# Two-layer decoder trunk on one core: FFN gate/up projection of steps 1 to 10 with the weights stationary and the tokens moving

## What is computed

```python
for l in range(2):
    x = x + 0.5 * swiglu(rmsnorm(x, norm_ffn1[l]), w1_gate[l], w1_up[l], w1_down[l])
    p = rmsnorm(x, norm_mix[l]) @ w_in[l]            # 1024 x 3072
    x = x + concat(diff_attention(p), retention(p)) @ w_out[l]
    x = x + 0.5 * swiglu(rmsnorm(x, norm_ffn2[l]), w2_gate[l], w2_up[l], w2_down[l])
return rmsnorm(x, norm_final)
# swiglu(h, g, u, d) = (silu(h @ g) * (h @ u)) @ d ;  g, u: 1024 x 2816 ;  d: 2816 x 1024
```

## Time and profile before

| | us |
|---|---|
| median of 3 runs | 993.77 (993.65 to 994.35) |
| profiled execution, first to last instruction (span) | 992.8 |
| TensorE busy in it | 965.0 (4512 matmuls) |
| VectorE / ScalarE busy | 547.3 / 455.8 |
| mean granted TensorE clock | 0.998 of full |

### The profile page before, as it was taken

One profiled execution on the slowest core, in us unless ns is written; L12 is line 12 of the kernel. 1 busy time (PEld: TensorE's weight loads), 2 busy tenths in 40 slices (PEclk: granted clock), 3 DMA queues, 4 the chain that ended last, 5 costly groups with the idle time before them and its releaser, 6 DMA issues.

```text
span 992.8 us, 12951 instructions
## 1 busy us (share of the span) xinstructions
PE 965.0 (97%) x4512; PEld 796.2 (80%) x4512; DVE 547.3 (55%) x628; ACT 455.8 (46%) x579; POOL 39.7 (4%) x73
## 2 busy tenths in 40 slices
PE   2999999999999999999999999999999999999997
PEld 2888888888888888888878888888888888888885
DVE  3654545565666645454655545456565755454454
ACT  3634344454573534343453434343655554343432
POOL 3400000000010000000000000000001000000000
PEclk9999999999999999999999999999999999999999
DMA  9664646447245655556536655656634645656541
GB/s 251 219 208 160 208 161 206 171 160 241 91 164 170 205 199 172 208 169 211 188 131 214 188 193 175 205 171 210 209 110 165 213 134 189 212 165 207 164 141 43
DMA packets 123179, 178.70 MB, mean 180 GB/s; under 512 B 5664, under 2 KB 95776, under 8 KB 123136
## 3 DMA queue, kind: packets, MB, share of 16 engines
q1 hardware_dynamic: 121808, 173.56, 52.4%
q0 software_dynamic: 1040, 3.54, 1.5%
q10 hardware_dynamic: 288, 1.05, 0.3%
HBM read 177.08 MB, written 1.05 MB: 179 GB/s over the span
## 4 chain that ended last, share of the span: by engine, by line
PE 95%; DMA 1%; ACT 1%; issue 1%; DVE 1%; SPq 0%; ACTq 0%; POOLq 0%; DVEq 0%; POOL 0%
PE gu L722 20%; PE gu L724 20%; PE gu L723 20%; PE acc L724 10%; PE acc L723 10%; PE acc L722 10%; PE tp L792 2%; DMA raw<-in_w_up_dram 1%; PE tp L737 1%; PE tp L840 1%; PE acc L851 1%; PE tp L863 1%; ACT w_hi L294 0%; ACT wide L394 0%; PE acc L863 0%
## 5 line engine op out<-in xcount | busy, mean ns | idle before, releaser
L478 DVE TENSOR_TENSOR w_lo<-raw,w_hi 128x2048 fp32r<-128x2048 f32 (+1 forms) x168 | 376.2, 2243 | 158.5 <-ACT w_hi L294 158.3
L722 PE MATMUL gu<-w_hi,xT_hi 128*128 128x512 f32 x896 | 353.1, 394 | 11.4 <-DVE w_lo L478 11.0
L724 PE MATMUL gu<-w_hi,xT_lo 128*128 128x512 f32 x896 | 350.2, 391 | 0.0
L723 PE MATMUL gu<-w_lo,xT_hi 128*128 128x512 f32 x896 | 349.7, 390 | 0.0
L294 ACT ACTIVATE w_hi<-raw 128x2048 fp32r<-128x2048 f32 (+1 forms) x168 | 313.8, 1872 | 21.8 <-DMA raw<-in_w_up_dram 11.4
L722 PEld LDWEIGHTS gu<-w_hi,xT_hi 128*128 128x128 f32 x896 | 168.8, 188 | 46.7 <-issue 12.3
L336 ACT ACTIVATE hid<-gu,st 128x256 f32<-128x256 f32 x88 | 41.8, 475 | 352.2 <-PE gu L724 352.1
L724 PEld LDWEIGHTS gu<-w_hi,xT_lo 128*128 128x128 f32 x896 | 168.7, 188 | 35.7
L723 PEld LDWEIGHTS gu<-w_lo,xT_hi 128*128 128x128 f32 x896 | 168.9, 189 | 34.1
L722 PE MATMUL acc<-w_hi,aT_hi 128*128 128x512 f32 x384 | 157.0, 409 | 0.0
L534 DVE SCALAR_TENSOR_TENSOR hid<-gu,st,hid 128x256 f32<-128x256 f32 x88 | 42.5, 483 | 205.3 <-ACT hid L336 205.3
(11 more groups left out here) (111 smaller groups left out, 396.4 us busy)
## 6 DMA issues: line engine op xcount, KB each, us to landing
raw<-in_w_gate_dram SPq DMA_DIRECT2D x88, 512.0 KB, 4.0
raw<-in_w_up_dram SPq DMA_DIRECT2D x88, 512.0 KB, 5.0
raw<-in_w_down_dram SPq DMA_DIRECT2D x88, 512.0 KB, 4.3
raw<-in_w_in_dram SPq DMA_DIRECT2D x40, 512.0 KB, 4.6
raw<-in_w_out_dram SPq DMA_DIRECT2D x16, 512.0 KB, 3.7
raw<-in_w_in_dram SPq DMA_DIRECT2D x16, 256.0 KB, 3.0
gain<-in_norm_ffn_dram POOLq DMA_DIRECT2D x3, 512.0 KB, 4.0
gain<-in_norm_mix_dram POOLq DMA_DIRECT2D x2, 512.0 KB, 4.8
```

The lines of the kernel that those rows point to most:

```text
L478: nc.vector.tensor_tensor(w_lo[:, pos % SLOTS, 0:n], raw[:, pos % RAW, 0:n], w_hi[:, pos % SLOTS, 0:n].bitcast(F32), ALU.subtract).then_in ...
L722: nc.tensor.matmul(out_, s_hi, m_hi, start=first, stop=False)
L723: nc.tensor.matmul(out_, s_hi, m_lo, start=False, stop=False)
L724: return nc.tensor.matmul(out_, s_lo, m_hi, start=False, stop=last)
```

## The change

In steps 1 to 10 the 128x128 blocks of the weights become the stationary operand and the 256 tokens move, so the results come out with the hidden columns on the partitions, as `down` needs them. Step 0 stays as it was, but for `rstd` on the up half.
- A piece now holds gate or up alone (all 1024 rows by 256 columns). `half_up` takes it in 2 blocks of 128 columns (`m`) by 8 row blocks (`k`): one matmul of `w_hi` with `xT_hi` and `xT_lo` side by side (512 moving columns) and one of `w_lo` with `xT_hi` (256 columns), the latter into columns 0 to 255 of the bank. Gate goes to the two `gu` banks, up to the two `tp` banks.
- The reader adds the halves of a bank: ScalarE copies columns 256 to 511, VectorE adds columns 0 to 255. As tokens are now on the free axis, gate is multiplied by `rstd` laid out as a row on all partitions, `r_bc`; up is not scaled at all.
- `r_bc` is made by GpSimd once for each FFN, by two DMAs through DRAM (`spread_rstd`). The missing factor comes in with the residual: `half_r = 0.5 * rstd` in place of 0.5.
- `hidden_T` goes in steps 1 to 10.

```diff
-                    if tt == 0:
-                        act.wait_ge(gu_ready, s_ + 1)
+                def step(s_, par, it, pos, nxt):     # ScalarE
+                    act.wait_ge(slot_free, SLOTS + LP * layer + SLOTS * it + base + pos + 1)
+                    nc.scalar.activation(gate_x, gu2[:, :, SEQ:], ACT.Copy).then_inc(gate_x_read, 1)
                     nxt(0)
-                    silu(s_, 1, it, pos)
-                    hidden_hi(2 * s_, par, 0)
+                    act.wait_ge(gate_scaled, w0 + s_ + 1)
+                    nc.scalar.activation(gate_r, gate_r, ACT.Silu).then_inc(wsilu_done, 1)
+                    act.wait_ge(slot_free, SLOTS + LP * layer + SLOTS * it + base + pos + 2)
+                    nc.scalar.activation(up_x, tp2[:, :, SEQ:], ACT.Copy).then_inc(up_x_read, 1)
+                    act.wait_ge(whid_done, w0 + s_ + 1)
+                    nc.scalar.activation(aT_hi[:, 2 * par:2 * par + 2, :], hiddenT, ACT.Copy).then_inc(wT_hi_done, 1)
                     nxt(1)
-                    hidden_hi(2 * s_ + 1, par, 1)
                     nxt(2)
...
+                def step(s_, par, it, pos, nxt):     # VectorE
+                    if pos == 2:
+                        dve.wait_ge(r_bc_loaded, 16 * i + 16)
+                        dve.wait_ge(hT_psum, 2 * i + 2)
+                    dve.wait_ge(gate_x_read, w0 + s_ + 1)
+                    nc.vector.tensor_tensor(gate_r, gu2[:, :, 0:SEQ], gate_x, ALU.add).then_inc(gate_summed, 1)
+                    dve.wait_ge(gate_summed, w0 + s_ + 1)
...
+                    nc.vector.tensor_tensor(by_tt, by_tt, r_bc[...], ALU.mult).then_inc(gate_scaled, 1)
+                    nxt(0)
+                    dve.wait_ge(up_x_read, w0 + s_ + 1)
+                    nc.vector.tensor_tensor(hiddenT, tp2[:, :, 0:SEQ], up_x, ALU.add).then_inc(up_summed, 1)
+                    dve.wait_ge(up_summed, w0 + s_ + 1)
+                    dve.wait_ge(wsilu_done, w0 + s_ + 1)
+                    nc.vector.tensor_tensor(hiddenT, hiddenT, gate_r, ALU.mult).then_inc(whid_done, 1)
+                    nxt(1)
+                    dve.wait_ge(wT_hi_done, w0 + s_ + 1)
+                    lo_of(aT_lo[:, ks, :], hiddenT, aT_hi[:, ks, :], wT_lo_done)
                     nxt(2)
...
+                def half_up(it, pos, banks, hook=None):     # TensorE
+                    piece_ready(layer, base + pos, it)
+                    slot = (base + pos) % SLOTS
+                    for m in range(2):
+                        for k in range(KT):
+                            if hook and (m, k) == (1, 0):
+                                hook()
+                            ws = slice(k * CH + m * P, k * CH + (m + 1) * P)
+                            nc.tensor.matmul(banks[m], w_hi[:, slot, ws], xT_both[:, k, :, :].rearrange("p h n -> p (h n)"),
+                                             start=k == 0, stop=False, skip_group_check=True)
+                            ins = nc.tensor.matmul(banks[m][:, 0:SEQ], w_lo[:, slot, ws], xT_hi[:, k, :],
+                                                   start=False, stop=k == KT - 1, skip_group_check=True)
+                    ins.then_inc(slot_free, 1)
...
+                    if hook is None:
+                        pe.wait_ge(gate_summed, w0 + s_)
+                    half_up(it, pos, gu, hook)
+                    if hook is None:
+                        pe.wait_ge(up_summed, w0 + s_)
+                    else:
+                        pe.wait_ge(hT_lo_done, 2 * i + 2)
+                    half_up(it, pos + 1, tp)
...
+                p_ = FFN_PIECES - 4
+                up(STEPS - 1, 0, p_)
                 for tt in range(TT):
-                    down(e - 2 + tt, 0, p_ + 2, 1, tt)
+                    down((wT_lo_done, w0 + STEPS - 1), 0, p_ + 2, 1, tt)
                     if tt:
                         enter_T(q + 1, 0)
-                    down(e + tt, 0, p_ + 3, 0, tt, last=True)
+                    down((wT_lo_done, w0 + STEPS), 0, p_ + 3, 0, tt, last=True)
...
+            def spread_rstd(layer, f):     # GpSimd
+                i = 2 * layer + f
+                pool.wait_ge(r_bc_loaded, 16 * i)
+                pool.dma_start(r_row, rstd).then_inc(r_row_stored, 16)
+                pool.wait_ge(r_row_stored, 16 * i + 16)
+                pool.dma_start(r_bc[:, :], r_row.rearrange("p t -> (p t)").partition_broadcast(P)).then_inc(r_bc_loaded, 16)
```

More of the change, by code:

```diff
@@ L86, in build @@
         ident = sb("ident", [P, P])
+        r_bc = sb("r_bc", [P, SEQ])
+        r_row = nc.dram_tensor("r_row", (P, TT), F32, kind="Internal").ap()
         lams = qT[:, 0:2, :].rearrange("p a (b n) -> p (a b) n", b=2)
@@ L273, in mixer_and_ffn2_entry @@
                     entry(3 * layer + 2, tt)
+                spread_rstd(layer, 1)
             next_gain(0, norm_mix[0, :])
@@ L365, in ffn @@
                 act.wait_ge(rstd_done, TT * (3 * layer + 2 * f) + TT)
-                step(s0, 0, 0, 1, pieces(0, 3, 4, None))
-                step(s0 + 1, 1, 0, 3, pieces(0, 5, 6, 7))
+                first_step(pieces(0, 3, 4))
+                step(1, 1, 0, 2, pieces(0, 5, 6, 7))
                 with act.Fori(0, LOOPED) as it:
@@ L370, in ffn @@
                         p_ = 8 + 3 * u
-                        step(s0 + 2 * it + 2 + u, u, it, 6 + 3 * u, pieces(it, p_, p_ + 1, p_ + 2))
-                step(s0 + STEPS - 1, 0, 0, FFN_PIECES - 3, last_lots)
+                        step(2 * it + 2 + u, u, it, 5 + 3 * u, pieces(it, p_, p_ + 1, p_ + 2))
+                step(STEPS - 1, 0, 0, FFN_PIECES - 4, last_lots)
             def head_squares(n, src, done):
@@ L510, in residual @@
                             dve.wait_ge(slot_free, SLOTS + used)
-                        nc.vector.scalar_tensor_tensor(x[:, tt, cols], acc[2 * tt + half][:, :], factor, x[:, tt, cols],
+                        by = 1.0 if factor == 1.0 else half_r[:, tt:tt + 1]
+                        nc.vector.scalar_tensor_tensor(x[:, tt, cols], acc[2 * tt + half][:, :], by, x[:, tt, cols],
                                                        ALU.mult, ALU.add).then_inc(x_new, 1)
@@ L543, in step, with first_hide @@
[L543 to L550, removed]
+                i = 2 * layer + f
+                w0 = (STEPS - 1) * i - 1
+                def first_hide(tt):
+                    dve.wait_ge(silu_done, 2 * i + tt + 1)
+                    nc.vector.tensor_tensor(hidden[:, tt, :], gu[tt][:, CH:2 * CH], silu_g[:, tt, :], ALU.mult).then_inc(hidden_done, 1)
@@ new lines, in first_lo, with first_step @@
+                def first_lo(tt):
+                    dve.wait_ge(hT_hi_done, 2 * i + tt + 1)
+                    lo_of(aT_lo[:, 0:2, tt * P:(tt + 1) * P], tp[tt][:, 0:CH].rearrange("p (k n) -> p k n", k=2),
+                          aT_hi[:, 0:2, tt * P:(tt + 1) * P], hT_lo_done)
+                def first_step(nxt):
+                    first_hide(0)
+                    nxt(0)
+                    first_hide(1)
+                    first_lo(0)
+                    nxt(1)
+                    first_lo(1)
@@ L563, in ffn @@
                 split_lo(layer, base + 2)
-                step(e0, 0, 0, pieces(0, 3, 4, None))
-                step(e0 + 2, 1, 0, pieces(0, 5, 6, 7))
+                first_step(pieces(0, 3, 4))
+                step(1, 1, 0, 2, pieces(0, 5, 6, 7))
                 with dve.Fori(0, LOOPED) as it:
@@ L568, in ffn @@
                         p_ = 8 + 3 * u
-                        step(e0 + 4 * it + 4 + 2 * u, u, it, pieces(it, p_, p_ + 1, p_ + 2))
-                step(e0 + 2 * (STEPS - 1), 0, 0, last_lots)
+                        step(2 * it + 2 + u, u, it, 5 + 3 * u, pieces(it, p_, p_ + 1, p_ + 2))
+                step(STEPS - 1, 0, 0, FFN_PIECES - 4, last_lots)
             def mixer(layer):
@@ L778, in ffn, with first_T @@
             def ffn(layer, f, base):
-                e0 = 2 * STEPS * (2 * layer + f)
+                i = 2 * layer + f
+                w0 = (STEPS - 1) * i - 1
                 q = 3 * layer + 2 * f
[L782 to L790, removed]
+                def first_T(tt):
+                    pe.wait_ge(hidden_done, 2 * i + tt + 1)
                     for k in range(2):
@@ L804, in ffn @@
+                project(layer, 0, 0, base, 2, gu_ready, lambda: enter_T(q, 1), q)
+                project(layer, 0, 1, base, 2, gu_ready, None, q)
+                first_T(0)
+                up(1, 0, 2, lambda: first_T(1))
                 for tt in range(TT):
-                    hidden_T(e0 + 2 + tt, tt)
-                    down(e0 + tt, 0, 4, 0, tt, first=True)
+                    down((hT_lo_done, 2 * i + tt + 1), 0, 4, 0, tt, first=True)
                 with pe.Fori(0, LOOPED) as it:
@@ L808, in ffn @@
                     for u in range(2):
-                        e = e0 + 4 * it + 4 + 2 * u
+                        s_ = 2 * it + 2 + u
+                        up(s_, it, 5 + 3 * u)
                         for tt in range(TT):
```

91 lines of the change are left out of this document (52 added, 39 removed).

## The result

The changed kernel takes **1016.59 us** (median of 4 runs, 1014.7 to 1017.46) against 994.06 for the kernel before (4 runs, 993.65 to 994.75): ratio 1.023, 95% interval 1.0213 to 1.0246. It is slower by 22.5 us. The prediction was 1007 us, range 993 to 1017, so the direction was right, the size was short by 9.6 us, and the time lies 0.4 us inside the range's upper end. The profiled execution has a span of 1014.8 us, 22.0 us over the span before.

What follows compares the result with a forecast made beforehand. TensorE, busy 97% of the span, was taken to bound the kernel. 993.8 - 18.2 (transposes) + 5.9 (gate and up matmuls) + 18.4 (end waits) + 7.2 (clock) = 1007 us, range 993 to 1017.

Steps and rivals of the forecast that it cites:

- The wait at the end: End of each FFN: TensorE waits for VectorE's `lo_of` of step 10, 5.8 us three times and 1.0 once, +18.4 us.
- The clock: After the three 5.8 us waits TensorE's clock has fallen and costs 2.4 us each to come back, +7.2 us.
- a late `r_bc`: In each FFN the `rstd` row arrives late for VectorE, up to 8 us more in all; chance 0.05.
- Transposes removed: Loop steps: 80 pairs of TensorE transposes go, each 0.227 us on the path, -18.2 us.
- The matmuls of gate and up: Loop steps: 1280 wide and 1280 narrow matmuls replace 1920 wide; a narrow one at 0.118 us, +5.9 us.
- Inside the loop, the start, `r_bc`: ScalarE, VectorE and DMA in the loop, and an FFN's start with the `rstd` row, cost TensorE no new time: 0.
- 1: Rival: the wait at an FFN's end is not there, 981.5 us, faster; chance 0.10.
- 3: Rival: a 256-column float32r matmul waits for its load's full 0.19 us, 91 us more, 1098 us; chance 0.04.
- 4: Rival: the row of `rstd` is late in each FFN, up to 8 us more, 1015 us; chance 0.05.
- Rival 2: Width fully sets a matmul's price (0.112 us narrow) and the clock holds: 992 us, with one 999 or 1000; chance 0.15.

Runs made afterwards that it cites:

- e1: The changed kernel with VectorE's `lo_of` of a step ahead of `nxt(1)` instead of behind it; 999.80 us, ratio 1.0061 to the kernel before.
- e2: e1, and at an FFN's end VectorE splits piece 33 after `lo_of` and piece 34 between the halves of the entry; 998.12 us, ratio 1.0049.
- e3: The changed kernel with 24 unread matmuls of 512 columns put into the wait after the first and third FFN; 1011.77 us, ratio 1.0189 to the kernel before.
- e4: e2 with a block's eight wide matmuls of `w_hi` ahead of its eight narrow ones of `w_lo`; 992.31 us, ratio 0.9992 to the kernel before.
- e5: e2 with the wide matmul of `w_hi` cut into two of 256 columns; 1006.43 us, ratio 1.0129 to the kernel before.

## Why the prediction was right, and where its size was off

The two terms that made the forecast "slower", the wait and the clock, came as they were worked out. That the time is inside the range at all is in part luck: the range's upper end allowed for a narrow matmul of 0.120 us, longer waits and a late `r_bc`, of which only the first came; what filled it instead is one term, 13 us over its forecast and outside its own ends. With the measured terms the sum is -20 + 19 + 17.6 + 6.9 = +23.5 us, against 22.5 measured.

- **The wait at the end** (forecast 5.8, 5.8, 5.8 and 1.0 us, 18.4 in all): 5.5 three times and 1.0, 17.6 in all. Its working went by the order of the lists and by durations of other operations of the same size, and each station came within 0.3 us: product to T + 2.8 (forecast 3.0), `hi` to 3.5 (3.7), split of 34 to 7.6 (7.9), `lo_of` to 8.2 (8.5). Shown by e1 and e2.
- **The clock** (forecast 2.4 us three times, 7.2): 6.9, for three waits and not for the fourth. The parts are uneven, 2.0, 2.0 and 2.9. Shown by e3. That the clock can fall after gaps of 1.4 and 1.8 us (e1) was not foreseen.
- **Transposes removed** (forecast -18.2): about -20. The stretch that was read, two matmuls either side, left out that the five matmuls behind it take up to 9 ns more each (150.55 to 151.71 is 1.16 us for them, where five of 226.7 ns are 1.13). Both ways of reading come from before; the step's period would have given it.
- **The matmuls of gate and up** (forecast +5.9, ends -2.1 and +8.6; with its own 0.112 us the lower end is -1.7): this is the term that failed. By the step, (16.80 - 24 x 0.2267) / 32 = 0.355 us a pair, the seam to the down matmuls with it, or 1280 x 0.355 - 1920 x 0.2267 = +19 us, outside the ends. The fixed part on top was right, 13.3 ns (e4, e5). Missing was the price of changing width: some 7 ns a pair when they alternate, and what it takes to get back to 226.7 behind them. Rows of before had the sign of it, in the matmuls behind the transposes.
- **Inside the loop, the start, `r_bc`** (forecast 0): 0. TensorE has no new wait there. The two DMAs for `r_bc` landed in 3.4 and 5.4 us at the median, and VectorE never waited for them.
- Of the rivals, 1 is out by the four waits of the changed kernel and by e1, 3 by the 120 ns of e5, 4 by the absence of any wait for `r_bc`. Rival 2 is out by e5 as to the price of the width and by the granted clock as to the clock. The gap rule of the Trainium skill ("TensorE: Matmul & The Clock Gate", Back-to-back issue gap), by estimate 109 ns for 256 columns, differs from what e5 shows, 120 ns; the measurement decides.

What stays open: why a wide float32r matmul behind a narrow one takes 6 to 15 ns more. The runs show when it is paid, not what pays it.

## What to carry to other kernels

When a result that came in two parts comes in one, look at the places where the first part was the cover for the second, above all where a loop ends and the next stage's preparations are squeezed in: what the waiting engine needs goes ahead of what merely is due. Price a mixed stream of matmuls from a mixed stream, or keep one width in long rows; the same matmuls in another order were worth 5.8 us. And count an idle time of TensorE of several microseconds with what the clock takes afterwards, here 2 to 3 us for each.

## What the runs showed that was not expected

- A float32r matmul has 13.3 ns on top of its columns at 2.4 GHz whether it has 512 or 256 of them (226.7 and 120.0 ns in a row). At 1.2 GHz wide ones stand 427 ns apart, just their columns, so nothing on top of them shows.
- Narrow and wide in turn take 353 ns a pair, where 347 would be the sum of the two in rows of their own.
- The clock fell in e1 after two idle times of 1.4 and 1.8 us with matmuls between them, and 1.2 us after TensorE had started again; in the waits for `lo_of` it fell within one idle time of 5.4 us.
